# The pooling's moving sums made by VectorE instead of GpSimd, and two hand-set tables set anew

## The reference, cut to what matters

```python
POOL_WINDOWS = (2, 4, 8, 16)
def pool_mixer(x, hist, pos0, w_grp, scale):
    ...
    for g, w in enumerate(POOL_WINDOWS):
        lo, hi = g * POOL_GROUP, (g + 1) * POOL_GROUP
        win = cs[:, ..., lo:hi] - cs[:, ... - w, lo:hi]     # cs: running sum over frames
        means.append(win / cnt)
    d = concatenate(means) - x
    y = einsum('bsgc,gcd->bsgd', d, w_grp) * scale
...
h = layer_norm(ALPHA * x + mixer(x));  r = relu(h @ w1);  f = (r * r) @ w2
x = layer_norm(ALPHA * h + f + (p @ ple_w) * sigmoid(h @ ple_gate_w))
```

## Time and profile before

| | |
|---|---|
| median of 3 runs | 2115.55 us (2115.45 to 2115.83) |
| the profiled execution | 2116.12 us, of which 2114.3 us span |
| granted TensorE clock, mean | 0.998 of full speed |
| busy: PE, DVE, ACT, POOL | 2103.8, 1267.3, 822.0, 73.2 us |

### The profile page before, as it was taken

How to read it: one execution, slowest core, us unless ns; L and a number is a source line. 1 busy time by engine, 2 the same in 40 slices (tenths; PEclk the granted TensorE clock), 3 DMA queues, 4 the chain that set the end, 5 groups by cost and what they waited for, 6 DMA issues and landing times.

```text
span 2114.3 us, 31844 instructions
## 1 busy us (share of the span) xinstructions
PE 2103.8 (100%) x13214; PEld 2101.1 (99%) x13214; DVE 1267.3 (60%) x1893; ACT 822.0 (39%) x1288; POOL 73.2 (3%) x67
## 2 busy tenths in 40 slices
PE   9999999999999999999999999999999999999998
PEld 9999999999999999999999999999999999999998
DVE  5233367886454444444787877887876355545477
ACT  4222223653423322222544445555443324333345
POOL 0000000000000000000020002000300000000000
PEclk9999999999999999999999999999999999999999
DMA  4010241444122111111122343543123212122233
GB/s 175 30 60 30 69 130 47 130 131 144 58 90 90 51 50 41 40 60 41 60 61 80 105 142 120 170 137 122 61 77 96 65 50 70 54 77 80 68 102 133
DMA packets 53777, 179.68 MB, mean 85 GB/s; under 512 B 8080, under 2 KB 10512, under 8 KB 53648
## 3 DMA queue, kind: packets, MB, share of 16 engines
q1 hardware_dynamic: 50624, 176.97, 25.7%
q10 hardware_dynamic: 3024, 0.88, 0.2%
HBM read 173.36 MB, written 4.46 MB: 84 GB/s over the span
## 4 chain that ended last, share of the span: by engine, by line
PE 99%; DVE 0%; DMA 0%; SPq 0%; issue 0%; ACT 0%; DVEq 0%
PE ps L696 33%; PE ps L697 33%; PE ps L698 33%; DMA x_raw<-x_t 0%; DVE acc L1185 0%; PE ps L757 0%; PE ps L756 0%; PE ps L725 0%; PE ps L731 0%; SPq L640 0%; PE ps L794 0%; PE ps L721 0%; SPq L652 0%; DVE x_lo L1325 0%; SPq L648 0%
## 5 line engine op out<-in xcount | busy, mean ns | idle before, releaser
L696 PE MATMUL ps<-h_hi,w_split 128*128 128x352 f32 x2160 | 696.9, 323 | 0.4 <-DVE acc L1278 0.4
L697 PE MATMUL ps<-h_lo,w_split 128*128 128x352 f32 x2160 | 691.9, 320 | 0.0
L698 PE MATMUL ps<-h_hi,w_split 128*128 128x352 f32 x2160 | 691.7, 320 | 0.0
L696 PE MATMUL ps<-r_hi,w_split 128*128 128x352 f32 x1634 | 526.8, 322 | 0.0
L697 PE MATMUL ps<-r_lo,w_split 128*128 128x352 f32 x1634 | 523.1, 320 | 0.0
L698 PE MATMUL ps<-r_hi,w_split 128*128 128x352 f32 x1634 | 522.8, 320 | 0.0
L1309 DVE TENSOR_TENSOR acc<-acc,ps 128x352 f32<-128x352 f32 (+1 forms) x769 | 372.8, 517 | 125.6 <-PE ps L698 124.9
L615 DVE TENSOR_TENSOR w_split<-w_raw,w_split 128x1024 fp32r<-128x1024 f32 x291 | 355.0, 1242 | 99.1 <-ACT w_split L886 98.4
L696 PEld LDWEIGHTS ps<-h_hi,w_split 128*128 128x128 f32 x2160 | 405.0, 188 | 1.1 <-issue 1.0
L697 PEld LDWEIGHTS ps<-h_lo,w_split 128*128 128x128 f32 x2160 | 405.9, 188 | 0.0
L698 PEld LDWEIGHTS ps<-h_hi,w_split 128*128 128x128 f32 x2160 | 404.8, 187 | 0.0
(11 more groups left out here) (132 smaller groups left out, 1198.6 us busy)
## 6 DMA issues: line engine op xcount, KB each, us to landing
w_raw<-w_stream SPq DMA_DIRECT2D x315, 512.0 KB, 3.5
x_raw<-x_t SPq DMA_DIRECT2D x4, 704.0 KB, 7.8
y_t<-acc SPq DMA_DIRECT2D x4, 704.0 KB, 4.0
w_raw<-p_t SPq DMA_DIRECT2D x6, 352.0 KB, 3.0
w_raw<-w_stream SPq DMA_DIRECT2D x3, 256.0 KB, 4.8
x_raw<-x_t SPq DMA_DIRECT2D x4, 176.0 KB, 4.0
x_raw<-x_t SPq DMA_DIRECT2D x2, 352.0 KB, 5.9
y_t<-acc SPq DMA_DIRECT2D x2, 352.0 KB, 2.2
```

The costliest lines, as they stand in the source:

```text
L696: pe.matmul(out, wh, mov_h, start=first, stop=False)
L697: pe.matmul(out, wh, mov_l, start=False, stop=False)
L698: return pe.matmul(out, wl, mov_h, start=False, stop=last)
```

## The change

The moving sum becomes a row of its own, `window_sum`, which stands after the fill and ahead of `centre_window` in the pooling's rows, and VectorE makes it. The same additions on the same buffers are done; GpSimd's loop goes. All lists of `PLACES` and `REFILL_LATER` are written anew: of the first, the two that place the norm and the pooling of pieces 1 and 2 are shown (the first 21 numbers are the norm's rows, the next 16, now 20, the pooling's). Of the 297 weight loads 32 are put off or brought forward by one or two steps or change places with a neighbour.

```diff
-    ('mlp', 0, 1): (225, 225, 227, 227, 228, 229, 229, 230, 230, 232, 233, 234, 237, 239, 239, 240, 240, 240, 241, 242, 242, 242, 242, 244, 244, 247, 249, 249, 252, 253, 254, 254, 257, 257, 257, 257, 259),
+    ('mlp', 0, 1): (225, 225, 227, 227, 228, 229, 229, 230, 230, 232, 233, 233, 236, 238, 238, 239, 240, 240, 241, 241, 241, 241, 241, 241, 244, 245, 246, 248, 249, 249, 252, 253, 254, 254, 254, 254, 256, 256, 257, 257, 259),
-    ('mlp', 0, 2): (284, 284, 284, 284, 286, 287, 287, 287, 287, 287, 287, 291, 292, 292, 292, 292, 294, 294, 296, 297, 297, 297, 297, 297, 297, 298, 300, 300, 300, 300, 300, 301, 301, 301, 303, 304, 305),
+    ('mlp', 0, 2): (284, 284, 284, 284, 286, 288, 288, 288, 288, 288, 288, 291, 292, 292, 293, 293, 294, 294, 296, 297, 297, 297, 297, 297, 297, 297, 298, 298, 298, 298, 298, 298, 300, 300, 301, 301, 301, 301, 303, 304, 305),
...
-            rows += [[("centre_window", 4 * n + q, 0)], [("centre_window", 4 * n + q, 1)]]
+            rows += [[("window_sum", 4 * n + q)], [("centre_window", 4 * n + q, 0)], [("centre_window", 4 * n + q, 1)]]
...
+                elif what == "window_sum":
+                    n, q = i // 4, i % 4
+                    end = WIN if n == NG - 1 else HIST + TG
+                    src, dst = wa[i % 2], wb[i % 2]
+                    dve.wait_ge(win_in, i + 1)
+                    lag, have = 1, 0
+                    while lag < WINDOWS[q]:
+                        have += lag
+                        ins = dve.tensor_tensor(dst[:, :, have:end], src[:, :, have:end], src[:, :, have - lag:end - lag], ALU.add)
+                        src, dst = dst, src
+                        lag *= 2
+                        if lag < WINDOWS[q]:
+                            then(ins)
+                    ins.then_inc(win_done, 1)
...
-            def window_sums(w):
...
-                pool.wait_ge(win_in, w + 1)
-
-                wait(pool, d_ready, w - 1)
...
-                    ins = pool.tensor_tensor(dst[:, :, have:end], src[:, :, have:end], src[:, :, have - lag:end - lag], ALU.add)
...
-            for step in plan:
-
-                for what, i, *rest in step.side:
-                    if what == "fill":
-                        window_sums(i)
```

More of the change, by code:

```diff
@@ L46 @@
 PLACES = {
[L47 to L50, removed]
@@ L51 @@
-    ('mix', 1, 0): (204, 204, 204, 206, 208, 208, 209, 209, 209, 210, 210, 210, 212, 212, 212, 213, 214, 216, 217, 217, 220, 220, 220, 224, 225),
-    ('mlp', 0, 1): (225, 225, 227, 227, 228, 229, 229, 230, 230, 232, 233, 234, 237, 239, 239, 240, 240, 240, 241, 242, 242, 242, 242, 244, 244, 247, 249, 249, 252, 253, 254, 254, 257, 257, 257, 257, 259),
-    ('mix', 1, 1): (261, 262, 263, 264, 265, 265, 267, 267, 268, 268, 270, 272, 273, 273, 273, 276, 277, 278, 280, 280, 281, 281, 282, 282, 282),
@@ L54 @@
-    ('mlp', 0, 2): (284, 284, 284, 284, 286, 287, 287, 287, 287, 287, 287, 291, 292, 292, 292, 292, 294, 294, 296, 297, 297, 297, 297, 297, 297, 298, 300, 300, 300, 300, 300, 301, 301, 301, 303, 304, 305),
-    ('mix', 1, 2): (305, 305, 306, 308, 309, 309, 312, 312, 312, 312, 313, 313, 314, 316, 316, 316, 318, 318, 319, 320, 322, 322, 323, 324, 326),
-    ('mlp', 1, 0): (357, 357, 357, 360, 361, 361, 361, 363, 364, 364, 365, 372, 375, 378, 382, 385, 385, 386, 393, 399, 400),
-    ('mlp', 1, 1): (433, 433, 434, 435, 436, 436, 436, 436, 440, 440, 441, 441, 443, 444, 448, 448, 452, 453, 454, 454, 455),
+    ('mix', 0, 0): (7, 8, 9, 9, 10, 10, 10, 10, 11, 11, 11, 12, 13, 14, 15, 16, 16, 16, 16, 16, 17, 17, 17, 19, 19),
@@ new lines @@
+    ('mix', 0, 1): (20, 20, 20, 21, 23, 23, 24, 25, 25, 26, 26, 26, 27, 28, 28, 28, 29, 29, 29, 29, 29, 30, 31, 31, 32),
+    ('mix', 0, 2): (32, 34, 35, 36, 37, 38, 39, 40, 40, 40, 40, 41, 44, 44, 45, 52, 55, 59, 63, 64, 64, 67, 73, 76, 82),
+    ('mlp', 0, 0): (181, 181, 182, 182, 184, 184, 185, 185, 185, 185, 185, 186, 188, 188, 188, 188, 192, 192, 192, 193, 193, 193, 193, 193, 194, 194, 196, 196, 196, 196, 198, 200, 200, 200, 200, 200, 202, 202, 202, 202, 204),
+    ('mix', 1, 0): (204, 204, 204, 205, 208, 208, 209, 209, 209, 209, 210, 210, 212, 212, 212, 213, 216, 216, 217, 217, 220, 220, 220, 224, 225),
@@ new lines @@
+    ('mlp', 0, 1): (225, 225, 227, 227, 228, 229, 229, 230, 230, 232, 233, 233, 236, 238, 238, 239, 240, 240, 241, 241, 241, 241, 241, 241, 244, 245, 246, 248, 249, 249, 252, 253, 254, 254, 254, 254, 256, 256, 257, 257, 259),
+    ('mix', 1, 1): (261, 261, 263, 264, 265, 265, 267, 267, 268, 268, 270, 272, 273, 273, 274, 277, 278, 279, 280, 280, 282, 282, 282, 282, 282),
+    ('mlp', 0, 2): (284, 284, 284, 284, 286, 288, 288, 288, 288, 288, 288, 291, 292, 292, 293, 293, 294, 294, 296, 297, 297, 297, 297, 297, 297, 297, 298, 298, 298, 298, 298, 298, 300, 300, 301, 301, 301, 301, 303, 304, 305),
@@ L58 @@
+    ('mix', 1, 2): (305, 305, 306, 308, 309, 309, 312, 312, 312, 312, 312, 313, 314, 314, 316, 317, 318, 318, 320, 321, 323, 323, 323, 324, 326),
+    ('mlp', 1, 0): (357, 357, 357, 360, 361, 364, 364, 364, 364, 364, 367, 372, 377, 380, 384, 385, 388, 389, 399, 405, 406),
+    ('mlp', 1, 1): (433, 433, 434, 435, 436, 436, 439, 439, 440, 440, 441, 441, 443, 444, 446, 448, 452, 452, 453, 454, 455),
     ('last', 1, 2): (449, 449),
@@ L1369, in _ @@
                 state(m)
[L1371 to L1377, removed]
-            def window_sums(w):
-                n, q = w // 4, w % 4
-                end = WIN if n == NG - 1 else HIST + TG
-                src, dst = wa[w % 2], wb[w % 2]
-                pool.wait_ge(win_in, w + 1)
-                wait(pool, d_ready, w - 1)
-                lag, have = 1, 0
-                while lag < WINDOWS[q]:
-                    have += lag
-                    ins = pool.tensor_tensor(dst[:, :, have:end], src[:, :, have:end], src[:, :, have - lag:end - lag], ALU.add)
[L1391 to L1395, removed]
-            for step in plan:
-                for what, i, *rest in step.side:
-                    if what == "fill":
-                        window_sums(i)
             pool.wait_ge(d_ready, NG * len(WINDOWS))
```

## The result

The changed kernel takes 2123.8 us (median of 7 runs, 2120.02 to 2124.22) against 2115.55 before. The prediction was 2122.0, range 2116.5 to 2124.0. The profiled execution took 2124.22, the highest value of the seven (two have it); its span is 8.1 us longer than that of the earlier trace rows.

A forecast was written before the change was run, and what follows sets the result against it. TensorE, busy 2103.8 of 2114.3 us, bounds the kernel. Costs of 0.1 + 1.95 + 3.0 + 1.6, less 0.04 waited today, give 6.6 us on the median of 2115.55: 2122.0 us, range 2116.5 to 2124.0.

The forecast's parts named there:

- The price of an addition: One moving-sum addition on VectorE: 0.94 us for 704 to 732 elements, 0.97 for 734 to 762.
- The cast's price: VectorE's 0.53 us for a cast of 704 elements, the nearest row from below for the price of an addition.
- GpSimd's slowing goes: Without GpSimd's 30 additions VectorE runs at undisturbed prices: two subtractions in piece 1 take 2.35 us instead of 3.79.
- Piece 0: Tiles 193 to 204: window 3's centring ends at 1096.0, its product is due at 1096.07; cost 0.1 us.
- Piece 1: Tiles 253 to 257: VectorE's sums delay tile 256's first block addition; TensorE waits about 1.95 us at tile 257.
- Piece 2: Tiles 297 to 301: VectorE's queue delays tile 300's first block addition; TensorE waits 3.0 us at tile 301.
- the rival of cheap additions: Additions at 0.57 us instead of 0.95: no wait in piece 1, ScalarE holds 1.9 in piece 2; 2117.4 us, chance 0.10.
- What costs nothing: The other moved rows of `PLACES` and the 32 moved weight loads make TensorE wait nowhere: no cost.
- The clock: TensorE's clock falls to its lower level once, behind piece 2's hole, costing 1.6 us; none behind piece 1's.
- more than that: Rival: both holes drop the clock, or one of the moved loads comes late; 2124 to 2126 us, chance 0.08.

The follow-up runs named there:

- the move of window 6: Changed kernel with window 7's fill and window 6's sums put behind tile 250, window 6's centring behind 253: 2120.87 us, ratio 1.0022.
- the kernel with both moves: Changed kernel with window 6 earlier, and window 10's sums, window 11's fill and the second half of window 9's centring later: 2116.01 us against 2115.71, ratio 1.0001.
- The two runs of piece 2's halves: Changed kernel with only window 10's sums, or only window 11's fill, moved from behind tile 298 to 300: 2122.77 us (1.0035) and 2123.08 us (1.0032).
- new tables, GpSimd: Changed kernel with both new tables, but all thirty additions back on GpSimd: 2125.68 us, ratio 1.0047.

## Why the prediction was right, and where it was not

- **The price of an addition**: 0.94 forecast; four take 3.74, 0.935 each, and one of 762 takes 0.944. The cast's price is out. By the errata table of the Trainium skill (VectorE: DVE Perf Modes, the TRN2 errata) 704 elements would take 0.79 by estimate; the section itself notes that this row is too low for single operations. The trace has 0.89, as the rows of the kernel before said.
- **GpSimd's slowing goes**: shown in the rows above (888 instead of 1159 ns; the two subtractions at 1294.52 take 2.36 instead of 3.79).
- **Piece 0**, 0.1: measured 0.08 at the product; the 0.4 us of slower matmuls behind it the working doesn't have. **Piece 1**, 1.95: measured 1.97, and the order that made it is shown by the move of window 6. **Piece 2**, 3.0: measured 2.95. The working left out a weight split that now stands ahead of window 8's sum (1.2 us on VectorE from 1481.95). It cost nothing, since `r_lo` of tile 298 still waited 0.23 for ScalarE; that was luck.
- Piece 2 was right in size with half of its cause: the working followed VectorE alone. ScalarE's chain over the fill of window 11 ends 0.15 earlier; the prediction had it only in the rival of cheap additions. With window 10's sums moved away this chain alone holds a wait of 2.68; that it would have held with cheaper additions too, as that rival said, was not tried.
- **What costs nothing**: the kernel with both moves, at 1.0001, shows no cost, to within some 2 us.
- **The clock**: the size of a fall came out (1.6 forecast, 1.7 and 1.6 measured), in part by luck: it was chosen between 0 and 2.3, and the 2.3 rests on matmuls at the start that were taken to be at the lower level. There the profile gives a clock of 1.00 (2 to 5 us), and three matmuls take 1.04; behind the first hole, at a clock of 0.50, three take 0.88 (1309.38 to 1310.26). The step that failed is the number of falls: "I take 1.6 once, [...] for piece 2 and none for the shorter hole of piece 1". In the profiled execution both holes drop the clock, which was the rival *more than that* (2124 to 2126, chance 0.08). The two runs of piece 2's halves show that a hole of 1.8 can be followed by a fall where one of 2.7 isn't. Without a fall the sum is 2115.55 + 0.1 + 1.97 + 2.95 = 2120.6, with one 2122.2, with two 2123.8; the seven runs lie at 2120.0, 2121.9, 2122.8 and four times at 2123.8 to 2124.2. So the median, 1.8 above the forecast, is what two falls would give, but only one of the seven has a trace, and how many falls the others had is not shown.
- **The range** holds the median by 0.2 us. It was meant to leave out most of the rival that the trace shows, so that it holds is luck.

What decides in a single execution whether the clock falls stays open. Nothing here was faster than the kernel before: both moves take back the loss, and TensorE has only the small waits of the earlier trace rows left to give.

## What to carry to other kernels

Work that goes to an engine with idle time is paid by whoever waits behind it in that engine's queue: find the next instruction in the queue that the bounding engine needs, and put the new work behind it, or into idle time ahead of it. Before a wait is put down to one queue, follow every input of the instruction that ends it: two chains here ended 0.15 us apart, and shortening either alone left the wait at 2.7 to 2.8 us. A table of places is set for the engines that it was made for; with the additions back on GpSimd the new one lost more than the change.

## What the runs showed of the hardware

- Holes of TensorE of 1.8 to 2.8 us between dense stretches are followed in most traces, not in all, by a stretch at a clock of 0.50 that loses some 1.6 us. It doesn't go by length: three of four waits of 1.8 have a fall behind them, and three of four of 2.7 to 2.8. The runs of the changed kernel are spread over 4.2 us, those of the kernel before beside it over 0.7 (in the later sets of its runs over 2.2 to 3.3); how much of the spread is the falls' is not shown.
- A fall can come while the engine still waits: in the wait of 7.1 us (new tables, GpSimd) the clock is 0.93 in 1490 to 1492 and 0.50 in the next stretch, with no matmul in either, and still 0.50 in 1498 to 1500, with TensorE busy throughout.

```profile
1490.00:1492.00 2.00, 0.00 (x0) 0.00 (x0) 1.97 (x2) 0.00 (x0) 1.84 (x2) 0.93 0.00 0
1492.00:1494.00 2.00, 0.00 (x0) 0.00 (x0) 0.74 (x2) 1.19 (x5) 0.00 (x1) 0.50 0.02 4
```
